# A decoder trunk with 32 experts on one core: an earlier issue of one slot's weights, and more dummy products ahead of the last sums

## The chip, the core and the metric

The kernel runs on one core of a Trainium2 chip. Its engines work side by side and meet at semaphores: TensorE (PE, products), VectorE (DVE), ScalarE (ACT), GpSimd (POOL) and SyncE (SP), which here only issues DMA transfers. ScalarE and GpSimd issue some too. The transfers of one core are carried by 16 DMA engines. The metric is the time of one execution on the device in microseconds (us); a smaller one is better.

## The reference

512 tokens of width 1024, in float32, with 16 learned meta tokens ahead of them, pass one layer. First come three parallel token mixers and an output product; then a mixture of experts; then a norm.

```python
u2 = _rmsnorm(h, norm_ffn[layer])
h = h + _hier_moe(u2, ...)
out = _rmsnorm(h, norm_final)

# _hier_moe: one of 4 groups, then 2 of its 8 experts for each token
p_group = softmax(xf @ wg + bg); g_val, g_idx = top_k(p_group, 1)
e_val, e_idx = top_k(softmax(e_logits of that group), 2)
combine = one_hot(group) * g_val * (e_val / sum(e_val))
for grp in range(N_GROUPS):
    hid = silu(xf @ w_gate[grp]) * (xf @ w_up[grp])       # 1024 -> 256, per expert
    y = y + sum over experts of combine * (hid @ w_down[grp])   # 256 -> 1024
```

Each expert has three matrices of 1 MiB each (gate, up, down), so 32 experts are 96 MiB.

## The kernel before

The mixers and the output product take the time up to about 820 us. What follows is the tail, written by hand for each engine; the order of instructions in the code is the order on the engine.

*Router.* For each of the four tiles of 128 tokens VectorE makes the normed tokens `u2`; SyncE stores tiles 0 to 2 to memory (`keep_rows`, L2045) and ScalarE the last one (L1737). All four count on the semaphore `rows_kept`. TensorE and VectorE then work out for each expert the list of its tokens, while TensorE also does dummy products (L1777).

*Experts.* GpSimd fetches the rows of two experts at a time from the stored tokens by indirect DMA (L2026; `fetch_pair`). TensorE turns a pair (L2066, counted on `pair_turned`), VectorE copies it (L2248), TensorE does the gate and up products (L2079, counted on `up_made`), and later the down products (L2088, counted on `made`). ScalarE copies the result, GpSimd sends it to `expert_results` (L2032).

*Weights.* There are six slots (`U = 6`), filled with experts 0 to 5 first; expert e goes to slot e % 6. SyncE issues gates (L2008) and ups (L2011) and some downs (L2018), ScalarE the other downs. SyncE's program is `esync`: the sixth slot's gate is issued early; its up matrix (which lies in the four lines of `gates` from 18 on) and its down matrix (`gates` lines 12 to 15) lie where the router's normed tokens were and are issued after the stored tokens. Behind them stand, in a loop, the gate and up of expert e + 6, each waiting until the up products of expert e are done. A wait in `esync` holds everything behind it on SyncE.

*End.* Eight transfers of 512 KiB bring the results back (L2522), two for each tile of tokens. TensorE first puts the old `h` into its sums (L2438), then runs dummy products of 128x128 (L2440) and then the products that weight and add the returned results (L2433): both halves of tile 1, the first halves of tiles 2 and 3. VectorE does the rest of the sums (L2457). ScalarE squares (L2486) and takes the root (L2491, L2493), VectorE writes the normed output (L2452) and SyncE stores it (L2525, L2528).

Of the kernel before, what the change touches and what calls it, by code (L numbers as in the profile page):

```python
# [104 lines left out]
def hybrid_trunk(nc, x, meta_tokens, norm_mix, w_in, hgrn_lb_logits, hgrn_norm, gdn_conv, gdn_a_log,  # L105
# [4 lines left out]
    with ctx:  # L110
# [5 lines left out]
        def sem(name):  # L116
            if name not in sems:
                sems[name] = ctx.enter_context(nc.semaphore(name))
            return sems[name]
# [46 lines left out]
        def bank(n, w=512):  # L166
            return ps[:, n * 512:n * 512 + w]
# [1502 lines left out]
        def tail():  # L1670
# [331 lines left out]
            pair_turned, pair_read = (Each(f"pair_{n}") for n in ("turned", "read"))  # L2002
# [4 lines left out]
            def load_gate(sp, n, e):  # L2007
                sp.dma_start(gate_and_up(n)[0], wgv[e]).then_inc(sem(f"expert_wu{n}"), 16)  # L2008

            def load_second(sp, n, e):  # L2010
                sp.dma_start(gate_and_up(n)[1], wuv[e]).then_inc(sem(f"expert_wu{n}"), 16)  # L2011

            def load_up(sp, n, e):
                load_gate(sp, n, e)
                load_second(sp, n, e)

            def load_down(sp, n, e):
                sp.dma_start(weights[n][1].rearrange("p (k d) -> p k d", k=2), wdv[e]).then_inc(sem(f"expert_wd{n}"), 16)  # L2018

            def load_weights(sp, n, e):  # L2020
                load_up(sp, n, e)
                load_down(sp, n, e)
# [13 lines left out]
            def esync(sp):  # L2036
                for n in (1, 2):
                    load_weights(sp, n, n)
                load_gate(sp, 4, 4)
                load_down(sp, 4, 4)  # L2040
                load_gate(sp, 5, 5)

                def keep_rows(i):
                    sp.wait_ge(*dve2.after(f"u{i}"))
                    sp.dma_start(u2_dram[i * P:(i + 1) * P, :], u2[:, i, :]).then_inc(sem("rows_kept"), 16)  # L2045
                for i in range(NT - 1):
                    keep_rows(i)
                sp.wait_ge(*pe2.after("o7"))
                load_weights(sp, 3, 3)
                load_second(sp, 4, 4)  # L2050
                sp.wait_ge(sem("rows_kept"), 16 * NT)
                sp.wait_ge(*pair_turned.of(0))
                load_second(sp, 5, 5)
                load_down(sp, 5, 5)
                for e in range(NX - U):
                    sp.wait_ge(*up_made.of(e))
                    load_up(sp, e % U, e + U)
                for e in range(NX - U - LATE, NX - U):
                    sp.wait_ge(*made.of(e))
                    load_down(sp, e % U, e + U)  # L2060
# [253 lines left out]
            for e, f in (("sync", esync), ("scalar", escalar), ("vector", evector), ("tensor", etensor), ("gpsimd", egpsimd)):  # L2314
                programs[e].append(f)
# [107 lines left out]
            def returned(eng, k, i):  # L2423
                eng.wait_ge(sem(f"results_back{k}{i}"), 16)

            def ftensor(t):
                def parts(i):
                    return (FIRST_HALF, SECOND_HALF) if i == 1 else (FIRST_HALF,)

                def choice(k, i):  # L2430
                    returned(t, k, i)
                    for lo, hi in parts(i):
                        mm = t.matmul(summed[i][:, lo:hi], choice_diag[:, k, i - 1, :], yg[2 * i + k][:, lo:hi], start=False, stop=(k == 1))  # L2433
                    return mm

                for i in (1, 2, 3):
                    for lo, hi in parts(i):
                        t.matmul(summed[i][:, lo:hi], ident, h[:, i, lo:hi], start=True, stop=False)  # L2438
                for _ in range(16):
                    t.matmul(bank(5, P), ones[:, :], ones[:, :], start=True, stop=True)  # L2440
                t.wait_ge(*fdve.after("dg1"))
                choice(0, 1)
                choice(1, 1).then_inc(*fpe.did("sum1"))
                choice(0, 2)
                choice(1, 2).then_inc(*fpe.did("sum2l"))
                choice(0, 3)
                choice(1, 3).then_inc(*fpe.did("sum3l"))
# [83 lines left out]
            for e, f in (("sync", fsync), ("scalar", fscalar), ("vector", fvector), ("tensor", ftensor)):  # L2531
                programs[e].append(f)
# [48 lines left out]
```

## Time and profile before

| | us |
|---|---|
| median of 3 runs | 1099.11 |
| lowest, highest | 1098.8, 1099.54 |
| the profiled execution | 1098.12 |
| its span, first to last instruction | 1096.3 |
| TensorE busy | 1047.3 (96%) |
| VectorE busy | 473.8 (43%) |
| ScalarE busy | 314.0 (29%) |

The mean granted TensorE clock of the profiled execution is 0.986. Busy shares are means over a span with different stages: up to about 820 us TensorE is the engine that never rests, while DMA stands at 40 to 120 GB/s for most of the time; in the experts the DMA engines move about 416 GB/s; the last 28 us are a chain of transfers, products and norms. So the stages are read one by one.

### The profile page before, as it was taken

The numbers are of one execution on the slowest core, as the hardware profiler recorded it, in microseconds if no ns is written. First come the engines' busy times: TensorE is split into PE (matmuls) and PEld (weight loads), VectorE is DVE, ScalarE is ACT, GpSimd is POOL, SyncE is SP. The second block draws the span as 40 slices with busy tenths as digits, with TensorE's granted clock in tenths as the row PEclk, the third lists the DMA queues.
The fourth block names the chain that finished last, engine by engine and source line by source line (L and its number), as shares of the span: only waits on it lengthen the run. The fifth ranks groups of instructions, "written<-read, shape, count | busy, mean of one in ns | idle before, by whom it ended". The sixth has DMA issues, their size and how long they took to land. (4 is left out here: it accounts for less than half of the span.)

```text
span 1096.3 us, 19207 instructions
## 1 busy us (share of the span) xinstructions
PE 1047.3 (96%) x8295; PEld 628.3 (57%) x8295; DVE 473.8 (43%) x973; ACT 314.0 (29%) x609; POOL 59.1 (5%) x69
## 2 busy tenths in 40 slices
PE   9999999999999999999999999999999999878796
PEld 7565655575575585585556556444555655534453
DVE  3646364638348347348254454423335321111123
ACT  2545445434324325325323033010110111101013
POOL 1000000000000000000000000000001222112110
PEclk9999999999999999999999999999999999989998
DMA  9422222233142142142212211054936999999976
GB/s 288 120 60 59 59 59 59 69 73 74 41 82 59 40 82 59 41 81 59 59 40 78 59 55 43 1 199 158 369 133 257 415 415 416 416 416 416 418 304 240
DMA packets 111959, 174.64 MB, mean 159 GB/s; under 512 B 9011, under 2 KB 87100, under 8 KB 103554
## 3 DMA queue, kind: packets, MB, share of 16 engines
q1 hardware_dynamic: 99010, 134.93, 35.5%
q10 hardware_dynamic: 7136, 27.33, 6.3%
q0 software_dynamic: 5728, 11.14, 4.1%
q8 instruction: 66, 1.08, 0.4%
q14 instruction: 19, 0.16, 0.0%
HBM read 169.16 MB, written 12.60 MB: 166 GB/s over the span
## 5 line engine op out<-in xcount | busy, mean ns | idle before, releaser
L694 PE MATMUL ps<-arena 128*128 128x512 f32 x672 | 314.3, 603 | 0.0
L694 PEld LDWEIGHTS ps<-arena 128*128 128x128 f32 x672 | 119.5, 190 | 112.3 <-issue 108.4
L691 PE MATMUL ps<-arena 128*128 128x264 f32 x416 | 128.3, 390 | 2.2 <-DVE lbc L289 1.4
L692 PE MATMUL ps<-arena 128*128 128x264 f32 x416 | 126.5, 386 | 0.0
L2079 PE MATMUL ps<-arena,gates 128*64 128x256 f32 x864 | 102.6, 392 | 22.6 <-DMA arena<-in_expert_w_up 21.1
L1310 DVE TENSOR_TENSOR arena<-arena 128x256 f32<-128x256 f32 (+6 forms) x194 | 92.0, 517 | 52.9 <-ACT arena L1106 33.5
L2079 PEld LDWEIGHTS ps<-arena,gates 128*64 128x64 f32 x864 | 62.7, 141 | 67.7 <-DMA arena<-in_expert_w_up 31.3
L685 PE MATMUL ps<-yT,arena 128*128 128x512 f32 x192 | 84.8, 596 | 2.1 <-DVE gates L1382 1.4
L692 PEld LDWEIGHTS ps<-arena 128*128 128x128 f32 x416 | 79.0, 190 | 13.5
L691 PEld LDWEIGHTS ps<-arena 128*128 128x128 f32 x416 | 75.9, 190 | 17.8 <-issue 6.3
L2248 DVE COPY gates<-ps 128x1024 f32<-128x1024 f32 x16 | 19.6, 1225 | 101.8 <-PE ps L2066 101.7
L685 PEld LDWEIGHTS ps<-yT,arena 128*128 128x128 f32 x192 | 35.7, 190 | 45.0 <-issue 44.6
L1770 PE MATMUL ps<-arena,gates 128*128 128x512 f32 x128 | 55.8, 592 | 0.0
L2163 ACT ACTIVATE gates<-ps 128x128 f32<-128x128 f32 x32 | 8.9, 278 | 143.1 <-PE ps L2079 143.1
L2088 PE MATMUL ps<-arena,gates 128*64 128x512 f32 x176 | 42.3, 604 | 0.0
L1770 PEld LDWEIGHTS ps<-arena,gates 128*128 128x128 f32 x128 | 24.0, 190 | 28.7 <-issue 28.2
L1314 DVE COPY_PREDICATED arena<-C,ps 128x512 f32<-128x512 int32 x56 | 39.6, 720 | 0.0
L2026 POOL DMA_INDIRECT gates<-normed_tokens,gates x16 | 16.6, 1037 | 423.9 <-DVE gates L1861 357.4
L2169 ACT ACTIVATE gates<-ps 128x512 f32<-128x512 f32 x32 | 19.1, 597 | 70.6 <-PE ps L2088 45.5
L2032 POOL DMA_INDIRECT expert_results<-gates x32 | 31.9, 997 | 122.7 <-ACT gates L2169 117.8
L2253 DVE TENSOR_TENSOR gates<-gates,ps 128x128 f32<-128x128 f32 x32 | 9.1, 284 | 63.9 <-ACT gates L2163 63.8
L760 PEld LDWEIGHTS ps<-arena 64*32 64x32 f32 x1824 | 19.1, 107 | 23.6 <-ACT arena L1230 12.1
(355 smaller groups left out, 1228.5 us busy)
## 6 DMA issues: line engine op xcount, KB each, us to landing
arena<-in_w_in SPq DMA_DIRECT2D x68, 512.0 KB, 3.8
arena<-in_expert_w_gate SPq DMA_DIRECT2D x27, 1024.0 KB
arena<-in_expert_w_up SPq DMA_DIRECT2D x27, 1024.0 KB
arena<-in_expert_w_down ACTq DMA_DIRECT2D x16, 1024.0 KB
arena<-in_w_branch SPq DMA_DIRECT2D x12, 512.0 KB, 4.0
arena<-in_expert_w_down SPq DMA_DIRECT2D x6, 1024.0 KB
C<-in_expert_w_gate SPq DMA_DIRECT2D x5, 1024.0 KB
gates<-in_expert_w_up SPq DMA_DIRECT2D x5, 1024.0 KB
```

The lines of the kernel that those rows point to most:

```text
L685: mm = t.matmul(merge_bank[b], wt, rhs, start=first, stop=last)
L691: t.matmul(dst[:, 0:HALF], wt, uT[:, k, 0:HALF], start=(k == 0), stop=(k == KD - 1))
L692: mm = t.matmul(dst[:, HALF:], wt, uT[:, k, HALF:], start=(k == 0), stop=(k == KD - 1))
L694: mm = t.matmul(dst, wt, uT[:, k, META:], start=(k == 0), stop=(k == KD - 1))
L760: mm = t.matmul(bank(n + h)[first:first + QUARTER, c * HP + q * QUARTER:c * HP + (q + 1) * QUARTER], lhs[rows, cs], rhs[rows, cs], start=T ...
L1310: v.tensor_tensor(out_, a_, b2, op).then_inc(*q.did(name))
L1314: v.copy_predicated(tiles(pm), over(up(l).bitcast(I32), NT), tiles(src)).then_inc(*q.did(name))
L1770: mm = t.matmul(bank(n), gates[:, k, i * P:(i + 1) * P], wo[:, k, n % 2 * 512:(n % 2 + 1) * 512], start=(k == 0), stop=(k == KD - 1))
L2032: return g.indirect_dma_start(out=y_dram, out_offset=bass.IndirectOffsetOnAxis(ap=which, axis=0), in_=rows, in_offset=None, bounds_check=4 ...
L2079: mm = t.matmul(dst, toks[:, k, :], src, start=(k == 0), stop=(k == KD - 1))
L2088: mm = t.matmul(bank(6 + b)[half * SLOTS:(half + 1) * SLOTS, :], hT[b][:, j * SLOTS:(j + 1) * SLOTS], weights[n][1][:, at:at + 512], start ...
L2248: v.tensor_copy(xT[q % 2], ps[:, 0:2 * 512].rearrange("p (k t) -> p k t", k=KD)).then_inc(pair_read.sem, 1)
```

## The change

SyncE no longer waits for the first turning ahead of the sixth slot's up and down matrices; the wait for the stored tokens stays. And the dummy products of 128x128 ahead of the last sums become 30 instead of 16. As one line is gone, lines behind L2052 have numbers lower by one in the changed kernel.

```diff
@@ -2049,7 +2049,6 @@
                 load_weights(sp, 3, 3)
                 load_second(sp, 4, 4)
                 sp.wait_ge(sem("rows_kept"), 16 * NT)
-                sp.wait_ge(*pair_turned.of(0))
                 load_second(sp, 5, 5)
                 load_down(sp, 5, 5)
                 for e in range(NX - U):
@@ -2436,7 +2435,7 @@
                 for i in (1, 2, 3):
                     for lo, hi in parts(i):
                         t.matmul(summed[i][:, lo:hi], ident, h[:, i, lo:hi], start=True, stop=False)
-                for _ in range(16):
+                for _ in range(30):
                     t.matmul(bank(5, P), ones[:, :], ones[:, :], start=True, stop=True)
                 t.wait_ge(*fdve.after("dg1"))
                 choice(0, 1)
```

SyncE's order around the first edit, before; `router_dve` counts the normed tokens, `pair_turned` the turned pairs, `expert_up` the up products:

```order
L2011 DMA arena<-in_expert_w_up 128x2048
L2018 DMA arena<-in_expert_w_down 128x2x1024
L2011 DMA arena<-in_expert_w_up 128x2048
L2011 DMA gates<-in_expert_w_up 128x2048 [waits pair_turned,rows_kept]
L2018 DMA gates<-in_expert_w_down 128x2x1024
L2008 DMA arena<-in_expert_w_gate 128x2048 [waits expert_up]
L2011 DMA arena<-in_expert_w_up 128x2048
```

And with the change:

```order
L2011 DMA arena<-in_expert_w_up 128x2048
L2018 DMA arena<-in_expert_w_down 128x2x1024
L2011 DMA arena<-in_expert_w_up 128x2048
L2011 DMA gates<-in_expert_w_up 128x2048 [waits rows_kept]
L2018 DMA gates<-in_expert_w_down 128x2x1024
L2008 DMA arena<-in_expert_w_gate 128x2048 [waits expert_up]
L2011 DMA arena<-in_expert_w_up 128x2048
```

No transfer changes its place in the row; the fifth one shown waits for one semaphore less.

TensorE's order at the end, before; `results_back` is a semaphore for each returned transfer:

```order
L2438 MATMUL ps<-yT,C 128x512 x4
L2440 MATMUL ps<-ones 128x128 x16
L2433 MATMUL ps<-arena,gates 128x512 [waits results_back01,final_dve]
L2433 MATMUL ps<-arena,gates 128x512
L2433 MATMUL ps<-arena,gates 128x512 [waits results_back11]
L2433 MATMUL ps<-arena,gates 128x512
L2433 MATMUL ps<-arena,gates 128x512 [waits results_back02]
```

And with the change:

```order
L2437 MATMUL ps<-yT,C 128x512 x4
L2439 MATMUL ps<-ones 128x128 x30
L2432 MATMUL ps<-arena,gates 128x512 [waits results_back01,final_dve]
L2432 MATMUL ps<-arena,gates 128x512
L2432 MATMUL ps<-arena,gates 128x512 [waits results_back11]
L2432 MATMUL ps<-arena,gates 128x512
L2432 MATMUL ps<-arena,gates 128x512 [waits results_back02]
```

The row of dummies grows from 16 to 30 and stays between the same neighbours; the products behind it wait for the same transfers as before.

## Rows read from the trace of the kernel before

**Rows 1.** The profile page's first line.

```profile
span 1096.3 us, 19207 instructions
```

**Rows 2.** Windows: stretch, length, busy by engine, clock, DMA share, GB/s.

```profile
830.50:835.50 5.00, 5.00 (x41) 2.55 (x41) 2.77 (x14) 0.00 (x0) 1.07 (x1) 1.00 0.00 2
835.50:840.50 5.00, 2.81 (x14) 1.55 (x14) 1.64 (x4) 0.00 (x0) 1.84 (x2) 1.00 0.43 119
840.50:845.50 5.00, 5.00 (x44) 3.76 (x43) 2.25 (x5) 0.28 (x1) 0.17 (x1) 1.00 1.02 400
...
918.00:1050.00 132.00, 106.30 (x804) 58.84 (x802) 21.57 (x56) 14.60 (x33) 24.99 (x25) 0.95 1.02 416
```

**Rows 3.** Timeline (start, length, engine, line, operation, tiles, count) of SyncE's issues.

```profile
838.93 0.33 SPq L2011 DMA_DIRECT2D gates<-in_expert_w_up  x1
...
844.03 0.33 SPq L2008 DMA_DIRECT2D arena<-in_expert_w_gate  x1
```

**Rows 4.** DMA issues: tiles, engine, count, size of each, median us to landing.

```profile
normed_tokens<-gates ACTq DMA_DIRECT2D x1, 512.0 KB, 8.6
```

**Rows 5.** Timeline of ScalarE's issues.

```profile
820.28 0.34 ACTq L1737 DMA_DIRECT2D normed_tokens<-gates  x1
```

**Rows 6.** DMA queues (packets, MB, share of 16 engines) from 838 to 845.4 us.

```profile
q1 hardware_dynamic: 349, 1.89, 66.3%
```

**Rows 7.** Timeline of GpSimd, the first and third gather; in brackets idle time before.

```profile
834.15 1.07 POOL L2026 DMA_INDIRECT gates<-normed_tokens,gates  x1 [357.38 <-DVE gates L1861]
...
839.68 0.99 POOL L2026 DMA_INDIRECT gates<-normed_tokens,gates  x1 [3.13 <-PE ps L2066]
```

**Rows 8.** DMA queues from 844 to 846 us: the gathers' queue.

```profile
q0 software_dynamic: 117, 0.21, 28.8%
```

**Rows 9.** Timeline of TensorE: first turning, last weight wait, and the end.

```profile
837.69 1.16 PE L2066 MATMUL ps<-C,gates 128*128 128x128 f32 x8 [0.72 <-DMA gates<-normed_tokens,gates]
...
1056.11 3.67 PE L2079 MATMUL ps<-arena,gates 128*64 128x256 f32 x32 [0.64 <-DMA arena<-in_expert_w_up]
...
1069.37 3.70 PE L2438 MATMUL ps<-yT,C 128*128 128x512 f32 x8
1072.91 3.73 PE L2440 MATMUL ps<-ones 128*128 128x128 f32 x32
1080.01 9.88 PE L2433 MATMUL ps<-arena,gates 128*128 128x512 f32 x16 [3.37 <-DMA arena<-expert_results]
```

**Rows 10.** Windows, as in rows 2: stretches that show the granted clock.

```profile
819.40:826.10 6.70, 6.70 (x15) 3.60 (x15) 5.38 (x22) 0.22 (x1) 0.00 (x0) 0.50 0.99 369
...
945.00:950.00 5.00, 3.56 (x42) 3.57 (x44) 0.00 (x0) 0.00 (x0) 0.99 (x1) 0.66 1.01 415
...
1072.91:1076.64 3.73, 3.73 (x33) 3.54 (x31) 0.00 (x0) 0.00 (x0) 0.00 (x0) 1.00 0.57 194
...
1078.80:1080.00 1.20, 0.00 (x0) 0.02 (x1) 0.86 (x1) 0.30 (x1) 0.00 (x0) 0.50 1.03 406
1080.00:1085.50 5.50, 5.49 (x7) 2.40 (x8) 3.10 (x4) 1.35 (x4) 0.00 (x0) 0.50 1.00 397
```

**Rows 11.** Timeline of ScalarE and VectorE at the end.

```profile
1085.11 0.75 DVE L2457 SCALAR_TENSOR_TENSOR yT<-arena,rw,yT 128x512 f32<-128x512 f32 x1 [0.44 <-DMA arena<-expert_results]
...
1086.49 1.02 ACT L2486 ACTIVATE gates<-ps 128x1024 f32<-128x1024 f32 x1 [5.08 <-PE ps L2433]
1088.20 1.28 DVE L2452 SCALAR_TENSOR_TENSOR yT<-ps,rw,gates 128x1024 f32<-128x1024 f32 x1 [2.34 <-ACT rw L2493]
...
1090.15 0.58 ACT L2486 ACTIVATE gates<-ps 128x512 f32<-128x512 f32 x1
...
1092.35 0.75 DVE L2452 SCALAR_TENSOR_TENSOR yT<-ps,rw,gates 128x512 f32<-128x512 f32 x1 [0.66 <-ACT rw L2493]
```

**Rows 12.** The return transfers: issue (ns; first and last start), and issue to landing.

```profile
L2522 SPq DMA_DIRECT2D arena<-expert_results x8: 352/437/920, 1073.3 to 1076.9; - x8
...
DMA to landing us min/median/max: 3.7/7.0/9.8
```

## The prediction

> **What bounds the kernel now.** I read the page's header first, then the stages by windows, then TensorE's waits, then the queues, and last the end of the span. The profiled execution took 1098.12 us, of which 1096.3 us are its span [rows 1]; the median of the timed runs is 1099.11 us, 1.0 us above. The windows show two different machines [rows 2]. From 918 to 1050 us the sixteen DMA engines are full (share 1.02, 416 GB/s) while TensorE works 106.3 of 132 us: the expert weights set the pace, and it still waits 0.64 us for an up matrix at 1056.11 us, the last such wait [rows 9]. Yet from 830.5 to 835.5 us the same engines move 2 GB/s, from 835.5 to 840.5 us 119 GB/s, and then 400 GB/s. That hole is what the first edit reaches into. The second edit lies in the final stage: TensorE ends its dummies at 1076.64 us (1072.91 + 3.73), stands idle 3.37 us until the results are back at 1080.01 us [rows 9], and does the products of 1080 to 1085.5 us at a granted clock of 0.50, which is 1.2 GHz; through the dummies themselves it was 1.00 [rows 10].
>
> **Edit 1, the wait that goes.** SyncE issued the two 1 MiB transfers at 838.93 us, held by the first turning [rows 3]. Without that wait only the stored tokens hold them. The last block of tokens was issued by ScalarE at 820.28 us [rows 5] and lands 8.6 us later [rows 4]: 828.9 us. So SyncE issues 10.0 us earlier. 2.10 MB at 400 GB/s are 5.2 us; they follow the transfers that run until about 830.3 us (the windows show the engines empty from 830.5 us) and are through by about 835.5 us, wholly inside the hole. Nobody queued behind them moves: the next issue is expert 6's gate at 844.03 us, released by the first up products [rows 3], and that wait stays.
>
> The naive worth is 2.10 MB at 416 GB/s, 5.0 us off a full DMA stage. I don't take it. What counts is what is still unsent when expert 6's weights begin to flow, because from there on the engines are full in both kernels. Issue to first data was about 1.3 us for the sixth slot (838.93 us, the engines pick up at about 840.3 us: at 400 GB/s from 840.5 us), so expert 6 flows from about 845.4 us. By then queue q1 had moved 1.89 MB since 838 us [rows 6], of 2.10 MB. Left are 0.21 MB, 0.5 us; with the rest of the third gather, some 0.04 MB that would have gone through idle engines, 0.6 us; the hole merely reopens at another place, from 840.5 us on. I take a gain of 0.7 us as the stream's start is known to 0.2 us only. Bound from the one side 5.0 us, from the other 0.
>
> **What it adds.** The first gather is issued by GpSimd at 834.15 us for 1.07 us [rows 7]; its data makes the first turn start at 837.69 us, and TensorE already waits 0.72 us for it [rows 9]. Everything behind it, expert 6's issue too, moves with it one for one. With the engines empty that took 3.54 us from the issue. The third gather, issued at 839.68 us with weights in flight [rows 7], moved its 0.21 MB only between 844 and 846 us [rows 8]: 6.3 us, 2.8 us later. So the new overlap costs between 0 and 2.8 us. The weights end at about 835.5 us and the gather's data starts after its issue ends at 835.22 us, so only the edge overlaps; nearest to the first gather's own row I take 0.3 us. Edit 1: 0.7 - 0.3 = 0.4 us gained; bounds 5.0 gained, 2.8 lost.
>
> The Trainium skill, "DMA: Bandwidth & Descriptors", section "Queues, rings and completion order", says that each DMA engine takes turns between the queues that have work, a packet at a time. By that rule a gather would hardly wait for weights in another queue and its lateness would be near 0; the third gather's row does not agree, since it took 6.3 us beside one queue of weights. By the rule edit 1 would be worth 0.7 us, by the row at its worst minus 2.1 us; the trace decides that the range must hold both.
>
> **Edit 2, 30 dummies for 16.** Before, 16 products are 32 records in 3.73 us [rows 9], 0.233 us each; 30 take 6.99 us and reach from 1072.91 to 1079.90 us, while the results come at 1080.01 us. Cost of the 14 added: nothing while the return transfers cover them, with 0.1 us to spare; if the data were early, each dummy too many costs 0.23 us. TensorE's idle time falls from 3.37 to 0.1 us, and I expect the clock to hold at 2.4 GHz.
>
> What that gives: the first tile of products (8 records) ended for ScalarE at 1086.49 us [rows 11]. Eight records of the same shape at full clock took 3.70 us [rows 9]: it would be 1083.71 us, 2.8 us earlier. Then something else is late. VectorE began the second tile's output 1.71 us behind ScalarE's start, at 1088.20 us [rows 11]; that would be 1085.42 us, but the half-row sum started at 1085.11 us holds VectorE until 1085.86 us, so the output runs until 1087.14 us. The eighth return transfer was issued at 1076.9 us and the longest landing is 9.8 us [rows 12]: 1086.7 us, which I ascribe to the last one. The last half sum on VectorE then ends at 1087.9 us, and the last product, a quarter of 3.70 us, at 1087.6 us. From ScalarE's last square of a product (1090.15 us) to VectorE's last-but-one output (1092.35 us) were 2.20 us [rows 11]: 1087.7 + 2.2 = 1089.9 us, 2.4 us earlier. The bound has passed from the products to the last transfer. The stores behind keep their distance. Below, the bound is nothing gained; above, 2.8 us.
>
> That is for a dip as long as the profiled one. The dips are not all alike: the one of 819.4 to 826.1 us holds 6.7 us at 0.50, and the one at the end is 0.50 from 1078.8 to 1085.5 us, as long, but 945 to 950 us has a mean of 0.66, so 3.4 us at 0.50 [rows 10]. With a dip of 3.4 us in the tail before, the first eight records lose 1.7 (half of 3.4) instead of 2.8 us, and the end gains 2.4 - 1.1 = 1.3 us. The timed runs don't show their dips; I take the middle, 1.8 us.
>
> The Trainium skill, "TensorE: Matmul & The Clock Gate", section "The HAM clock gate (the "warmup" mystery)", says that the instant of a clock change varies from run to run as the chip's look at activity is not tied to the kernel. No row here shows two runs. By it alone the gain would be anywhere between the two values of the paragraph before, not fixed at 2.4 us.
>
> **Sum.** In the profiled run's own terms 0.4 + 2.4 = 2.8 us, 1098.12 to 1095.3 us, if the dip was as in the profile. For the median of timed runs 0.4 + 1.8 = 2.2 us: 1099.11 - 2.2 = 1096.9 us. A difference under 0.2%, 2.2 us, is what a measurement of this kernel can't tell from none; the forecast stands on that edge.
>
> **Rivals.**
> A, the forecast: the clock holds, the first gather is late by little: 1096.9 us, its own range 1095.8 to 1098.0 us. Chance 0.64; half of it is beyond 0.2%.
> B, the gather pays: the first gather behaves as the third did, 2.8 us late. For: both had weights in flight near them. Against: the weights end before its data would start. Edit 1 then loses 2.8 - 0.7 = 2.1 us and edit 2 gives 1.8: 0.3 us slower than before, 1099.4 us. Chance 0.13.
> C, the other side: dummies don't hold the clock. Place: the stretch behind 1076.64 us. For: from 819.4 to 826.1 us TensorE was busy 6.70 of 6.70 us at a clock of 0.50 [rows 10], behind narrow products, so busy is not enough. Against: 3.73 us of dummies had 1.00. Price: the clock falls where it fell before, at 1078.8 us at the latest [rows 10]; 9 of the 14 added dummies are done, 5 at 0.466 us end at 1081.1 us, 1.1 us behind the data, and the products stay slow: 1.1 - 0.4 = 0.7 us slower, 1099.8 us. It decides from the point where more than 0.1 us of the added dummies runs at 0.50. Chance 0.09.
> D, the full 5.0 us: edit 1 takes all its bytes out of the full stage, because expert 6's weights flow as soon as the queue is free. Against: their issue is held by the up products of expert 0. 1099.11 - 5.0 - 1.8 = 1092.3 us. Chance 0.05.
> E, no dip to save: the timed runs, or most of them, had no slow products in the tail before. For: the dips of [rows 10] differ in length, so some may be missing. Against: 3.37 us of idle time stand in the profile, and it has one. Edit 2 gives nothing, edit 1 its 0.4 us: 1098.7 us. Chance 0.09.
>
> **Chances.** Faster by over 0.2%: half of A, D, and a little of the others with a long dip: 0.41. Slower by over 0.2% needs B and C together or dearer than priced: 0.05. Within: 0.54. The range leaves out D and the far side of B and C: 1095.4 to 1099.3 us.
>
> **What would show it.** Edit 1: SyncE's two issues at about 829 us; 400 GB/s between 830.5 and 835.5 us; a thin stretch from 840.5 us; the first turn at 837.7 to 838.1 us; the full stage ending 0.4 us sooner, not 5. A first turn after 839 us shows B; PE waits shortened by 5 us in sum show D. Edit 2: a clock of 1.00 from 1072 to 1088 us, the 16 records in about 7.5 us instead of 9.88 with small waits for transfers, ScalarE's square of the second tile about 3.7 us behind the first product. A clock of 0.50 inside the dummies shows C. If the clock holds and the end of the span moves under 1 us against that product, the tail's bound was mis-sized.

## The result, and the profile after

The change makes the kernel slower. Over 20 executions of each, the median is 1103.61 us with the change and 1099.26 us without, 4.35 us more; the ratio of the runs is 1.0032 with a 95% interval of 1.0018 to 1.0046. The forecast was 1096.9 us, with a range to 1099.3 us, so it was wrong in sign. The 20 executions of the kernel before lie between 1095.4 and 1107.5 us: the three shown at first (1098.8 to 1099.5 us) agreed by luck.

The profiled execution of the changed kernel took 1105.78 us; its span is 1104.0 us, 7.7 us more than that of [rows 1]. The stages by windows, columns as in [rows 2]:

```profile
830.50:835.50 5.00, 5.00 (x43) 3.29 (x42) 2.52 (x7) 1.49 (x2) 0.00 (x0) 1.00 1.00 397
835.50:840.50 5.00, 5.00 (x30) 2.25 (x26) 1.96 (x11) 0.00 (x0) 2.08 (x2) 1.00 0.90 360
840.50:845.50 5.00, 1.20 (x9) 0.97 (x8) 0.00 (x0) 0.00 (x0) 0.00 (x0) 1.00 0.40 152
...
918.00:1050.00 132.00, 112.30 (x806) 63.15 (x806) 23.45 (x60) 14.60 (x33) 24.26 (x24) 0.92 1.02 416
```

From the fourth slot on everything lies 5.2 us later in this execution than in the profile before, so the windows must be shifted before they are compared. The first stretch above still carries the earlier slots' weights, as the kernel before did until about 830.3 us. What answers to the hole of [rows 2] (2 GB/s from 830.5 to 835.5 us) is 835.7 to 840.7 us, nearly the second stretch: 360 GB/s. So the hole is filled, as the edit has it, but a new one opens behind it: 152 GB/s in the third stretch, in which TensorE works only 1.20 of 5 us, and 34 GB/s from 845.9 to 852.6 us, in a window shown below. TensorE's timeline and those of SyncE and GpSimd say why; they answer to [rows 3, 7, 9]:

```profile
821.27 0.33 SPq L2008 DMA_DIRECT2D arena<-in_expert_w_gate  x1
...
834.21 0.33 SPq L2011 DMA_DIRECT2D gates<-in_expert_w_up  x1
834.58 0.44 SPq L2018 DMA_DIRECT2D gates<-in_expert_w_down  x1
853.45 0.33 SPq L2008 DMA_DIRECT2D arena<-in_expert_w_gate  x1
```

```profile
837.71 1.07 POOL L2026 DMA_INDIRECT gates<-normed_tokens,gates  x1 [355.41 <-DVE gates L1861]
```

```profile
844.29 1.16 PE L2065 MATMUL ps<-C,gates 128*128 128x128 f32 x8 [3.76 <-DMA gates<-normed_tokens,gates]
846.93 6.49 PE L2078 MATMUL ps<-arena,gates 128*64 128x256 f32 x32 [1.48 <-DVE gates L2247]
...
1078.93 3.70 PE L2437 MATMUL ps<-yT,C 128*128 128x512 f32 x8
1082.47 6.86 PE L2439 MATMUL ps<-ones 128*128 128x128 f32 x60
1090.09 6.28 PE L2432 MATMUL ps<-arena,gates 128*128 128x512 f32 x14 [0.76 <-DMA arena<-expert_results]
1096.68 1.12 PE L2432 MATMUL ps<-arena,gates 128*128 128x512 f32 x2 [0.31 <-DMA arena<-expert_results]
```

The weights go out at 834.21 us, the first gather 3.50 us behind them, and the first turning starts 6.58 us after the gather's issue (3.54 us before). TensorE waits 3.76 us instead of 0.72, its clock falls to 1.2 GHz, and the first up products take 6.49 us instead of 3.67. At the end the dummies reach the results but for 0.76 us, and the 16 records take 7.7 us, a wait of 0.31 us among them, instead of 9.88 us. The clock in windows, to be read against [rows 10]:

```profile
845.90:852.60 6.70, 5.67 (x28) 3.58 (x30) 3.12 (x6) 0.00 (x0) 0.99 (x1) 0.50 0.13 34
1090.10:1096.30 6.20, 6.20 (x14) 2.46 (x14) 3.87 (x5) 3.13 (x11) 0.00 (x0) 1.00 1.00 403
```

The queues, from 834 to 841 us and from 841 to 844.3 us (packets, MB, share):

```profile
q1 hardware_dynamic: 458, 2.47, 90.4%
q0 software_dynamic: 3, 0.01, 0.4%
...
q0 software_dynamic: 283, 0.48, 39.4%
q1 hardware_dynamic: 26, 0.06, 4.4%
```

The gathers' queue q0 moved 0.01 MB while the weights ran, and 0.48 MB, which are the first two gathers together, once they had drained.

Three sections of the span and what lies ahead of them sum up to the difference. *Front*: fourth slot's gate issued to expert 6's gate issued. *Stage*: from there to the first record of L2438. *Tail*: from there to the end. Before: 28.0, 225.3, 26.9 us. After: 32.2, 225.5, 25.1 us. Between these two executions the change costs 4.2 us in the front, nothing in the stage, and gives 1.9 us in the tail. The two fronts aren't alike, though: the one before holds 6.8 us of half clock in the router [rows 10], the one after 3.4 us. The experiments below show what that hides. The other 5.2 us lie ahead of the fourth slot (816.04 against 821.27 us), where both programs are the same; of the eleven kernels below seven reach it between 821 and 823 us.

### The profile page after: what moved, and what is told of

Same layout as the page of the kernel before. It is cut to its first block and busy times, and to the rows that moved or that the text cites. A ratio compares the mean times of both kernels' runs of the same rounds, so it can differ in the third digit from the quotient of the medians.

```text
span 1104.0 us, 19262 instructions
## 1 busy us (share of the span) xinstructions
PE 1056.1 (96%) x8323; PEld 635.6 (58%) x8323; DVE 473.6 (43%) x973; ACT 314.2 (28%) x609; POOL 59.0 (5%) x69
## 5 line engine op out<-in xcount | busy, mean ns | idle before, releaser
L2078 PE MATMUL ps<-arena,gates 128*64 128x256 f32 x864 | 108.2, 407 | 17.1 <-DMA arena<-in_expert_w_up 15.6
L2078 PEld LDWEIGHTS ps<-arena,gates 128*64 128x64 f32 x864 | 65.3, 147 | 64.7 <-DMA arena<-in_expert_w_up 25.4
## 6 DMA issues: line engine op xcount, KB each, us to landing
arena<-in_expert_w_gate SPq DMA_DIRECT2D x27, 1024.0 KB, 27.6
```

Of the source, the lines that this page charges most:

```text
L2078: mm = t.matmul(dst, toks[:, k, :], src, start=(k == 0), stop=(k == KD - 1))
```

## The experiments

Each ran beside the kernel before, 9 to 12 executions each against 29 to 35. The ratio given is not that of the two medians; with so few executions the two can lie 1 to 2 us apart, and what is called shown goes by the ratio's interval. Theory T1 is that the early weights delay the first gather and let the clock fall; T2 that the dummies cost the time.

**Edit 1 alone.**

```diff
 # the change, with
-for _ in range(30):
+for _ in range(16):
```

> Edit 1 with the old 16 dummies. Theory T1 (the sixth slot's weights are in flight when the first gather is issued, the gather lands some 3 us late, and the clock falls in TensorE's wait): first gather issued to first turning 6 to 7 us instead of 3.5, first up products above 5 us instead of 3.67, time 5 to 6 us above before. Rival T2 (the gather has nothing to do with it, the 30 dummies or their end cost the time): gather to turning 3.5 us, time within 1 us of before.

Median 1104.65 against 1100.33 us, ratio 1.0053 (1.0030 to 1.0077): edit 1 alone carries a loss as large as the change's, so T2 falls. But the profiled execution is not of the kind T1 foretold. SyncE, GpSimd, TensorE:

```profile
833.82 0.33 SPq L2011 DMA_DIRECT2D gates<-in_expert_w_up  x1
```

```profile
839.27 1.07 POOL L2026 DMA_INDIRECT gates<-normed_tokens,gates  x1 [357.17 <-DVE gates L1861]
```

```profile
842.78 1.16 PE L2065 MATMUL ps<-C,gates 128*128 128x128 f32 x8 [0.69 <-DMA gates<-normed_tokens,gates]
```

Windows of the router, of the tail's idle time, and of the products behind it:

```profile
824.40:831.20 6.80, 6.80 (x15) 3.70 (x16) 5.39 (x22) 0.22 (x1) 0.00 (x0) 0.50 1.00 370
...
1081.90:1085.40 3.50, 0.00 (x0) 0.00 (x0) 2.57 (x2) 0.49 (x1) 0.00 (x0) 1.00 0.99 368
1085.50:1091.70 6.20, 6.20 (x14) 2.42 (x14) 3.81 (x5) 3.50 (x12) 0.00 (x0) 1.00 1.00 397
```

Here the clock was at half for 6.8 us in the router, as in the profile before; the router was late, the gather was issued 5.45 us behind the weights, and it took 3.51 us: no delay, just what was predicted. The front is 28.0 us, as before. So the loss depends on how long the router ran at half clock, which varies from execution to execution. The tail shows the same chance: TensorE was idle for 3.5 us with the old 16 dummies, and yet the clock stayed at 1.00.

**Edit 2 alone.**

```diff
 # the kernel before, with
-for _ in range(16):
+for _ in range(30):
```

> Edit 2 alone, the wait for the first turning back in place. T1: the front is as before (3.5 us from gather to turning), the products at the end run at full clock and the time is 1 to 2.5 us under before. T2: 4 us slower than before, as the whole change.

Median 1098.86 against 1100.33 us, ratio 1.0000 (0.9979 to 1.0020). The medians lie 1.5 us apart, as T1 had it, but the interval holds no difference. In its profile the clock never fell in the router, and the front is 25.0 us, 3.0 us less than before: this is what a router without half clock is worth, and what edit 1 spoils: with the early weights and an equally quick router the front is 30.9 us (from ScalarE's queue, below).

**Weights behind the first gather.**

```diff
 # the change, with
+sp.wait_ge(sem("pair_x0"), 16)
 load_second(sp, 5, 5)
```

> Both edits, but the sixth slot's two weights wait until the first gather has landed: earlier than before by the turning (1.3 us), later than in the change. T1: gather to turning 3.5 us, no fall of the clock at the start, the time 1.5 to 3 us under before. Rival T3 (any early weights hurt, the second and third gathers count too): time between before and the change, 1 to 3 us above before.

Median 1098.47 us, ratio 0.9991 (0.9970 to 1.0013); 3.53 us from gather to turning, no fall at the start. The loss is gone: this interval and the change's (1.0018 to 1.0046) don't meet. T1 stands; of T3's 1 to 3 us above before the interval leaves only the edge, up to 1.4 us, and the profile shows no delay. Its router had the long half clock, front 28.0 us.

**Clock kept in the wait.**

```diff
 # the change, with (four more products of 512 columns behind the slots' table)
-keep_busy(5)
+keep_busy(9)
```

> The whole change with 4 more dummy products of 512 columns (3.4 us) at the end of the router, so that TensorE isn't idle while it waits for the late gather. T1: gather still 3 us late, but the first up products take 3.67 us, not 6.5: 2.5 to 3 us faster than the change, about 1 us above before. Rival T4 (the clock fall costs nothing because the full DMA stage swallows it): same time as the change, 4 us above before.

Median 1101.21 us, ratio 1.0010 (0.9990 to 1.0031), against 1.0032 of the change. The timelines:

```profile
835.17 1.07 POOL L2026 DMA_INDIRECT gates<-normed_tokens,gates  x1 [354.68 <-DVE rw L1864]
```

```profile
841.73 1.16 PE L2065 MATMUL ps<-C,gates 128*128 128x128 f32 x8 [0.30 <-DMA gates<-normed_tokens,gates]
844.37 3.67 PE L2078 MATMUL ps<-arena,gates 128*64 128x256 f32 x32 [1.48 <-DVE gates L2247]
```

The weights had gone at 832.62 us, 2.55 us ahead. The gather is as late as in the change (6.56 us), but the up products keep 3.67 us. So of the 5.9 us between gather and expert 6 (15.74 us from issue to issue in the change, 9.88 before), 3.0 are the gather's and 2.8 the clock's. The intervals of this ratio and the change's overlap, so the time points to T1 but doesn't rule out T4; the two timelines are what speaks for the 2.8 us.

**Only 1 MiB early.**

```diff
 # the change, with
 load_second(sp, 5, 5)
+sp.wait_ge(*pair_turned.of(0))
 load_down(sp, 5, 5)
```

> The change, but only 1 MiB (the up matrix) goes early; the down matrix waits for the first turning again. Theory F (the gather's data flows only when the weights issued before it have drained): weights drain about 4 us after their issue, so with 3.5 us between the two issues the gather takes 3.5 to 4.2 us to the turning, with 2.5 us between them up to 4.8 us; no fall of the clock at the start; time within 1.5 us of before. Rival P (any weight traffic at the gather's issue costs a fixed 3 us): 6.5 us to the turning whenever the gap is under 3 us, time 3 to 4 us above before.

Median 1100.39 against 1098.80 us, ratio 1.0001 (0.9982 to 1.0019). The gap was 2.33 us and the gather took 4.17 us: half the bytes, 0.6 us of delay in place of 3.0. F holds, P falls. That the clock wouldn't fall was a miss: TensorE waited 1.35 us, then 1.48 us more for VectorE's copy, and the clock fell at 844.1 us, the up products taking 5.09 us. Whether the short delay caused this isn't shown: a profile below has such a fall with no early weights at all.

**Weights together with the gather.**

```diff
 # the change, with (released with the first gather's list)
+sp.wait_ge(*dve2.after("xo"))
 load_second(sp, 5, 5)
```

> The change, but both weights are held until the first gather's list is ready, so that they are issued at the same moment as the gather or a little before. Theory F: the gather's data waits for all or most of the 2 MiB, 6 to 9 us to the turning, a clock fall at the start, time 5 to 8 us above before. Rival R (the DMA engines take turns between queues): under 5 us to the turning, time within 2 us of before.

Median 1105.84 us, ratio 1.0054 (1.0035 to 1.0074). SyncE, GpSimd and TensorE:

```profile
835.68 0.33 SPq L2011 DMA_DIRECT2D gates<-in_expert_w_up  x1
```

```profile
836.55 1.07 POOL L2026 DMA_INDIRECT gates<-normed_tokens,gates  x1 [354.25 <-DVE gates L1861]
```

```profile
844.38 1.73 PE L2066 MATMUL ps<-C,gates 128*128 128x128 f32 x8 [5.01 <-DMA gates<-normed_tokens,gates]
```

Gap 0.87 us, 7.83 us to the turning: F holds, R falls. The nearer the weights are ahead of the gather, the longer it takes. Here the two did overlap a little: from 841 to 842 us q0 moved 0.13 MB beside 0.28 MB of weights, but nothing from 836.5 to 841 us.

**From ScalarE's queue.** The two early transfers move from `esync` to the head of `escalar` (three lines of code written as one here):

```diff
-sp.wait_ge(sem("rows_kept"), 16 * NT); load_second(sp, 5, 5); load_down(sp, 5, 5)
+a.wait_ge(sem("rows_kept"), 16 * NT); load_second(a, 5, 5); load_down(a, 5, 5)
```

> The change, but the sixth slot's two early transfers are issued by ScalarE on its queue behind the stored tokens. Theory F (the backlog is in the shared engines, whatever the queue): as the change, gather 3 us late when the gap is under 4 us, time 3 to 5 us above before. Rival Q (it is SyncE's queue that shuts the gather out): 3.5 us to the turning and the time 1 to 3 us under before.

Median 1103.50 us, ratio 1.0041 (1.0021 to 1.0060); gap 2.32 us, gather 6.50 us, up products 6.50 us. With the weights on the other queue the gather is as late as in the change (6.58 us) and q0 moved 0.02 MB up to 840 us; Q falls.

**45 dummies at the end**, in the kernel before.

```diff
-for _ in range(16):
+for _ in range(45):
```

> Before with 45 dummies at the end. They need 45 x 0.229 = 10.3 us where the results take 7.1 us: the products begin 3.2 us late but at full clock, and catch up with the last returned transfer by their own slack of about 2 us. Expected 1 to 2 us above edit 2 alone, about as before. Rival (the clock does not need the cover): 3 us above before.

Median 1102.00 us, ratio 1.0012 (0.9990 to 1.0034), the interval too wide to place it against edit 2 alone; one of the 12 executions took 3723 us, which nothing here explains. The profile:

```profile
1075.76 10.21 PE L2440 MATMUL ps<-ones 128*128 128x128 f32 x90
1085.80 7.03 PE L2433 MATMUL ps<-arena,gates 128*128 128x512 f32 x16
```

No wait is left ahead of the products, and the tail is 27.0 us against 25.1 us with 30: 1.9 us for 3.35 us more of dummies, within what was expected. The rival isn't refuted: the median lies 3.2 us above before, the interval allows anything from 1.1 us less to 3.7 us more, and edit 1 alone had a tail of 24.8 us with 16 dummies and no fall.

**A later router.**

```diff
 # the change, with (four more dummy products ahead of the rank products)
-keep_busy(6)
+keep_busy(10)
```

> The change with 4 more dummy products (3.4 us) ahead of the rank products, so that the first gather is always issued later. Theory G (the loss hangs on the time between the weights' issue and the gather's): this time becomes 5 to 6.5 us in every clock case, the gather takes 3.5 us to the turning, the first up products 3.67 us, and the kernel with 3.4 us of added work is no slower than the change, 1 to 3 us faster. Rival H (the early weights cost something else too): gather or up products as in the change and the time 3 us above it.

Median 1099.96 against 1100.50 us, ratio 0.9994 (0.9973 to 1.0014). The gather is issued 6.99 us behind the weights, later than the 5 to 6.5 us foretold, and needs 3.42 us; the up products take 3.67 us:

```profile
834.57 0.33 SPq L2011 DMA_DIRECT2D gates<-in_expert_w_up  x1
```

```profile
841.56 1.07 POOL L2026 DMA_INDIRECT gates<-normed_tokens,gates  x1 [359.01 <-DVE gates L1861]
```

```profile
844.98 1.16 PE L2065 MATMUL ps<-C,gates 128*128 128x128 f32 x8 [0.60 <-DMA gates<-normed_tokens,gates]
```

With 3.4 us of useless work added, the kernel is not slower than the change but faster (the intervals don't meet). So the loss hangs on the gap between the two issues: G holds, H, which asked for 3 us above the change, falls.

**A dense product among narrow ones**, with edit 2, and then also with the weights behind the first gather.

```diff
 # edit 2 alone, with (ahead of the last four turnings of tokens)
+keep_busy(1)
 turn_tokens(3, high_half, "T3b")
```

> Edit 2 alone with one dense dummy product (0.86 us) between the narrow logit products of the router. Theory D (the clock falls there because the products are narrow): no fall there in the profile, 25 to 26 us from the fourth slot's issue to expert 6's instead of 28, median 1 to 2 us under edit 2 alone. Rival (one product is too little, or the fall comes by chance): a fall as before and the time 0.9 us above edit 2 alone.

> As the last, with the sixth slot's weights held only until the first gather has landed. Theory: as the last, within 0.5 us, since the stage of full DMA keeps its length from expert 6's issue on. Rival: 1 us faster, from weights sent 1.3 us sooner.

Medians 1098.48 and 1098.57 against 1100.50 us, ratios 0.9990 (0.9970 to 1.0009) and 0.9984 (0.9962 to 1.0006). The clock did not fall in the router of either, as D says, but it hadn't in edit 2 alone, so two profiles prove little. In the first it fell at 838.8 us instead, behind TensorE waits of 0.79 and 1.48 us, and the up products took 5.34 us, so the front is 27.6 us and not the 25 to 26 foretold; the second has a front of 25.8 us. Nor is the gain of 1 to 2 us over edit 2 alone shown; the ratios' intervals overlap. These are the lowest ratios of the study, and neither interval excludes no change. No version is shown to beat the kernel before.

All profiles side by side, in us; each is one execution, read off the same timeline rows as above. "Half clock in the router" is how long the granted clock stood at 0.50 there:

| kernel | half clock in the router | gap, weights to gather | gather to turning | first up products | front | stage | tail |
|---|---|---|---|---|---|---|---|
| before | 6.8 | none ahead | 3.54 | 3.67 | 28.0 | 225.3 | 26.9 |
| after | 3.4 | 3.50 | 6.58 | 6.49 | 32.2 | 225.5 | 25.1 |
| edit 1 alone | 6.8 | 5.45 | 3.51 | 3.67 | 28.0 | 225.5 | 24.8 |
| edit 2 alone | 0 | none ahead | 3.49 | 3.67 | 25.0 | 225.6 | 25.1 |
| behind first gather | 6.8 | none ahead | 3.53 | 3.67 | 28.0 | 225.5 | 25.3 |
| clock kept | 0 | 2.55 | 6.56 | 3.67 | 28.1 | 227.3 | 25.2 |
| 1 MiB early | 0 | 2.33 | 4.17 | 5.09 | 27.1 | 225.7 | 24.6 |
| with the gather | 0 | 0.87 | 7.83 | 5.64 | 31.9 | 227.2 | 24.6 |
| ScalarE's queue | 0 | 2.32 | 6.50 | 6.50 | 30.9 | 225.8 | 24.4 |
| 45 dummies | 0 | none ahead | 3.50 | 3.67 | 25.0 | 225.6 | 27.0 |
| later router | 3.4 | 6.99 | 3.42 | 3.67 | 29.6 | 225.2 | 24.5 |
| dense product | 0 | none ahead | 3.61 | 5.34 | 27.6 | 226.7 | 25.6 |
| dense, behind gather | 0 | none ahead | 3.51 | 3.67 | 25.8 | 227.0 | 24.7 |

Read like with like, the front costs more than the 4.2 us of the first comparison: with no half clock in the router it is 25.0 us without early weights and 30.9 us with them on ScalarE's queue, 5.9 us more; with 6.8 us of half clock it is 28.0 us either way, nothing more.

## Why the prediction was wrong

*Edit 1, the hole.* This step failed: "The weights end at about 835.5 us and the gather's data starts after its issue ends at 835.22 us, so only the edge overlaps". Each time in it held in an execution like the profiled one (edit 1 alone: gap 5.45 us, no delay): the tokens landed 8.7 us after their issue (8.6 predicted), and the weights took 5 us. But the gap between tokens landed and gather issued, 5.25 us there, is no constant of the kernel. It was so long because 6.8 us of half clock from 819.4 us on [rows 10] slowed the router, and with it the gather's issue, but not the stored tokens; I read that row only as a fact on dummies and on the length of falls. With 3.4 us of it the gap is 3.5 us, with none 2.3 to 2.6 us, and then the gather stands behind the weights. Of the eleven profiles with this stretch of the router unchanged, six show no fall, two the short one and three the long one. The prediction took the one case in which the edit is harmless for the only one. An estimate from these rows: a cost of 5.9 us in eight of eleven executions is 4.3 us on average; edit 1 alone measured 4.3 us by medians and 3.3 to 8.5 us by its interval. Eleven profiles are few for such a share.

*Edit 1, the price.* Rival B was this mechanism, and its 2.8 us was near (3.0 measured). Its sum was not: it left out that TensorE's clock falls in or behind the wait of 3.76 us, another 2.8 us. And the third gather's 2.8 us was no upper bound: with the weights 0.87 us ahead the first gather was 4.3 us late (7.83 against 3.54 us).

*Edit 1, the gain.* The 0.7 us that the full stage should give are not there: from expert 6's issue to the end of the experts it takes 225.2 to 225.8 us in nine of thirteen profiles, with the sixth slot's weights sent or not; the other four, all at 226.7 to 227.3 us, had a fall of 6.8 us between 1016 and 1029 us. That the rest is timed by expert 6's issue, and that the naive 5.0 us are not to be had, was right; rival D is out.

*The turns between queues.* By the rule of the Trainium skill, "DMA: Bandwidth & Descriptors", section "Queues, rings and completion order", the gather would have had its turns beside the weights. The queues' rows and three experiments don't agree here: q0 moved 0.01 to 0.02 MB while the weights ran, beside weights of either queue; and with a gap of 2.3 us the turning came 6.50 us after the gather's issue behind 2 MiB and 4.17 us behind 1 MiB. The prediction weighed the rule and the row and took a value near the rule.

*Edit 2.* In the changed kernel's profile the clock held and the dummies ended 0.76 us ahead of the results; rival C is out. The end of the chain moved 1.9 us (26.9 to 25.1 us), in the forecast's 1.3 to 2.4; the last transfer landed 10.1 us after its issue and the last products waited for it, as said. The value for timed runs is uncertain. The clock held ahead of the last products in all eleven profiles with 30 or 45 dummies, but with 16 it fell in one of two: edit 1 alone had no fall and a tail of 24.8 us. So rival E may be true in part, and the 1.9 us of the profiles may be luck of the one before. Edit 2 alone shows no gain outside its interval (2.3 us less to 2.2 us more), which holds the forecast's 1.8 us too: neither shown nor refuted.

*The noise.* Three runs within 0.7 us were taken for the kernel's spread. It is 12 us; half clock here and there makes at least a part of it, as the 3.0 us between fronts and some 1.5 us between stages show.

## What to carry to other kernels

A free stretch in a profile is a number of one execution: before putting transfers into it, ask which clock state made it and how long it is in the others. A small gather that everything waits for is to be kept clear of bulk transfers issued shortly ahead of it: here 2 MiB issued 3.50 us ahead made it 3.0 us late, and 5.45 us ahead not at all. Put behind its landing, they showed no cost (ratio 0.9991), and no gain beyond the interval either. What a late transfer costs is its delay and what the engine's clock loses in the wait.

## What the runs showed of the hardware

- The first of two indirect gathers, 0.50 MB together, took 3.4 to 3.6 us from issue to use with no weights issued less than 5 us ahead of it, 6.5 to 6.6 us with 2 MiB of weights issued 2.3 to 3.5 us ahead, 7.8 us at 0.9 us ahead, and 4.2 us with 1 MiB 2.3 us ahead. Nearly all of their bytes came when the weights had drained, whichever of two queues held them. Why, the traces don't tell.
- The same stretch of instructions shows no, 3.4 or 6.8 us of half clock at one place (products of 36 columns) in different executions: six, two and three of eleven. At the end, with 16 dummies ahead, the clock fell in an idle time of 3.4 us in one profile and not in one of 3.5 us in another.
